# Loading three heads' results, the small columns and the function table of the output stage before the block boundary

## What is computed

```python
_, o = lax.scan(step, s0, xs)                  # recurrence over chunks, 16 value heads of 128
o = o.transpose(1, 0, 3, 2, 4).reshape(bsz, t, nh, dh)
o = rms_norm(o, norm_w) * jax.nn.silu(z.reshape(bsz, t, nh, dh).astype(f32))
y = o.reshape(bsz, t, nh * dh).astype(h.dtype) @ w_out
...
x = x + gate[:, None, :] * y
return rms_norm(x, final_g)
...                                            # second layer:
h = _rmsnorm(x, norm_pre[l])
```

## Time and profile before

| | us |
|---|---|
| median of 3 runs | 2101.82 |
| lowest and highest of them | 2099.18, 2102.6 |
| the profiled execution, its own time | 2103.15 |
| its span in the profile | 2101.4 |
| mean granted clock of TensorE in it | 0.985 |
| last write of the scan (L781) starts | 917.54 |
| first instruction of the second block | 919.88 |

### The profile page before, as it was taken

How to read it: one execution, slowest core, us unless ns; L and a number is a source line. 1 busy time by engine, 2 the same in 40 slices (tenths; PEclk the granted TensorE clock), 3 DMA queues, 4 the chain that set the end, 5 groups by cost and what they waited for, 6 DMA issues and landing times.

```text
span 2101.4 us, 29428 instructions
## 1 busy us (share of the span) xinstructions
PE 1992.7 (95%) x11256; PEld 1618.2 (77%) x11256; DVE 1272.9 (61%) x2415; ACT 853.5 (41%) x1376; POOL 138.4 (7%) x114
## 2 busy tenths in 40 slices
PE   4989999999999999969998999999999899999998
PEld 2667878888887878857776787777777678888877
DVE  6777777797869686749635644445353435633543
ACT  5644353544345443159403333544443337600321
POOL 0030202021111212000000000000000000000000
PEclk8999999999999999989999999999999999999999
DMA  7222233232323242548213211120312125211232
GB/s 282 86 75 70 87 89 106 65 101 71 105 68 105 67 120 68 168 158 287 80 41 136 66 60 41 41 101 21 111 41 81 61 72 219 91 49 41 85 116 80
DMA packets 128971, 200.27 MB, mean 95 GB/s; under 512 B 56596, under 2 KB 88084, under 8 KB 127808
## 3 DMA queue, kind: packets, MB, share of 16 engines
q1 hardware_dynamic: 128832, 198.39, 29.6%
HBM read 156.22 MB, written 42.11 MB: 94 GB/s over the span
## 4 chain that ended last, share of the span: by engine, by line
PE 47%; DVE 4%; DMA 2%; issue 2%; ACT 1%; SPq 0%; DVEq 0%; ACTq 0%
PE m_job L1682 6%; PE m_job L1684 6%; PE m_job L1683 6%; PE e_b L2369 4%; PE e_b L2371 4%; PE e_b L2370 4%; PE p_out L1352 2%; PE p_out L1353 2%; PE p_out L1354 2%; PE p_sc L1928 2%; PE p_s L1951 2%; PE e_b L2440 1%; PE e_b L2438 1%; PE e_b L2439 1%; DMA m_raw<-in_w 1%
## 5 line engine op out<-in xcount | busy, mean ns | idle before, releaser
L795 PE MATMUL p_job<-h_hi,w_hi 128*128 128x512 f32 x768 | 322.0, 419 | 18.8 <-DVE h_lo L185 17.3
L797 PE MATMUL p_job<-h_hi,w_lo 128*128 128x512 f32 x768 | 302.9, 394 | 0.0
L796 PE MATMUL p_job<-h_lo,w_hi 128*128 128x512 f32 x768 | 302.3, 394 | 0.0
L1682 PE MATMUL m_job<-h_hi,m_hi 128*128 128x512 f32 x576 | 237.6, 413 | 5.3 <-issue 4.2
L1684 PE MATMUL m_job<-h_hi,m_lo 128*128 128x512 f32 x576 | 227.4, 395 | 0.0
L1683 PE MATMUL m_job<-h_lo,m_hi 128*128 128x512 f32 x576 | 226.4, 393 | 0.0
L795 PEld LDWEIGHTS p_job<-h_hi,w_hi 128*128 128x128 f32 x768 | 146.0, 190 | 59.5 <-issue 16.2
L796 PEld LDWEIGHTS p_job<-h_lo,w_hi 128*128 128x128 f32 x768 | 146.1, 190 | 35.4 <-issue 7.9
L797 PEld LDWEIGHTS p_job<-h_hi,w_lo 128*128 128x128 f32 x768 | 145.8, 190 | 31.4
L1682 PEld LDWEIGHTS m_job<-h_hi,m_hi 128*128 128x128 f32 x576 | 108.8, 189 | 52.5 <-issue 31.0
L633 ACT ACTIVATE pre<-p_job 128x512 f32<-128x512 f32 x96 | 56.7, 591 | 179.1 <-PE p_job L797 179.1
(11 more groups left out here) (395 smaller groups left out, 4166.3 us busy)
## 6 DMA issues: line engine op xcount, KB each, us to landing
w_raw<-in_w SPq DMA_DIRECT2D x49, 512.0 KB
m_raw<-in_w SPq DMA_DIRECT2D x49, 512.0 KB, 3.8
rows<-grows SPq DMA_DIRECT2D x32, 512.0 KB, 6.6
ada<-in_ada_w SPq DMA_DIRECT2D x8, 1024.0 KB, 5.3
z_scr<-pre SPq DMA_DIRECT2D x16, 512.0 KB, 2.6
o_scr<-oT SPq DMA_DIRECT2D x64, 128.0 KB, 1.8
ob<-o_scr SPq DMA_DIRECT2D x16, 512.0 KB, 4.8
zb<-z_scr SPq DMA_DIRECT2D x16, 512.0 KB, 4.8
```

Source lines behind the costliest of these rows:

```text
L795: nc.tensor.matmul(bank, hi, h_hi[:, k, cut], start=(k == 0), stop=False)
L796: nc.tensor.matmul(bank, hi, h_lo[:, k, cut], start=False, stop=False)
L797: last = nc.tensor.matmul(bank, lo, h_hi[:, k, cut], start=False, stop=(k == KD - 1))
L1682: nc.tensor.matmul(bank, hi, h_hi[:, k, cut], start=(k == 0), stop=False)
```

## The change

`ob`, `nw`, `fg` and `np_col`, and the semaphores that count their loads, move from `stage_out` into `keep`, so that they exist in both blocks. SyncE issues the loads of `ob` for heads 0, 1 and 2 and of the three columns in the last pass of the first block, at `("merge", 0)`, behind a wait for the stores of heads 0 to 3. In the output stage the first `ob` load is that of head 3; the wait for all stores stands behind the first `zb` load. The table load at the head of `stage_out` (L1252) goes; ScalarE asks for the same table in the last pass behind the write of the last chunk but one. The SBUF reserved for descriptors, which takes its room from the same memory, is set to 1024 bytes per partition; before, the size wasn't given.

```diff
@@ stage_deltanet, SyncE's walk over the plan
+                        elif s[0] == "merge" and not s[1] and i == QK_HEADS:
+                            for q in range(2):
+                                sp.wait_ge(o_stored[q], 16 * NT)
+                            for m in range(3):
+                                sp.dma_start(keep["ob"][:, m, :], io["o_scr"][m]).then_inc(keep["o_in"][m], 16)
+                            for n, src in (("nw", "norm_w"), ("fg", "final_g"), ("np_col", "norm_pre")):
+                                sp.dma_start(keep[n][:], io[src]).then_inc(keep["cols_in"], 16)
@@ stage_deltanet, ScalarE, step "write"
                             nc.scalar.activation(oT[:, c % 2], p_query, ACT.Copy).then_inc(o_done, 1)
+                            if m == NT * QK_HEADS - 2:
+                                nc.scalar.preload_act_table_set(EXP_LN)
@@ stage_out
-        ob = sb("ob", [P, 3, T])
+        ob, nw, fg, np_col = (keep[n] for n in ("ob", "nw", "fg", "np_col"))
-        nw = sb("nw", [P, 1])
-        fg = sb("fg", [P, KD])
-        np_col = sb("np_col", [P, KD])
-        cst = sem("c_cst"); x_in = sem("c_x"); o_in = [sem(f"c_o{q}") for q in range(3)]; ...
+        cst = keep["cols_in"]; x_in = sem("c_x"); o_in = keep["o_in"]; ...
@@ stage_out, SyncE
-            load_o(0)
-            load_o(1)
-            sp.wait_ge(keep["o_stored"], 16 * QK_HEADS * NT // 2)
-            for dst, src in ((nw, io["norm_w"]), (fg, io["final_g"]), (np_col, io["norm_pre"])):
-                sp.dma_start(dst[:], src).then_inc(cst, 16)
             for m in range(len(steps)):
                 if m < V_HEADS:
                     if m >= 3:
                         sp.wait_ge(ylo_done, m - 2)
                     sp.dma_start(zb[:, m % 3, :], io["z_scr"][m]).then_inc(z_in[m % 3], 16)
-                if 2 <= m + 1 < V_HEADS:
+                if m == 0:
+                    sp.wait_ge(keep["o_stored"], 16 * QK_HEADS * NT // 2)
+                if 3 <= m + 1 < V_HEADS:
                     load_o(m + 1)
                 load_w(m)
@@ stage_out, ScalarE
-            nc.scalar.preload_act_table_set(EXP_LN)
@@ build and kernel
+            "ob": sb("ob", [P, 3, T]), "nw": sb("nw", [P, 1]), "fg": sb("fg", [P, KD]), "np_col": sb("np_col", [P, KD]),
+            "o_in": [ctx.enter_context(nc.semaphore(f"o_in{q}")) for q in range(3)],
+            "cols_in": ctx.enter_context(nc.semaphore("cols_in")),
-    nc = bacc.Bacc("TRN2", target_bir_lowering=False, num_devices=1)
+    nc = bacc.Bacc("TRN2", target_bir_lowering=False, num_devices=1, dynamic_dma_scratch_size=1024)
```

More of the change, by code:

```diff
@@ L1184, in y @@
             return middle[:, n - KD, :] if n < KD + 2 else high[:, n - KD - 2, :]
-        cst = sem("c_cst"); x_in = sem("c_x"); o_in = [sem(f"c_o{q}") for q in range(3)]; z_in = [sem(f"c_z{q}") for q in range(3)]
+        cst = keep["cols_in"]; x_in = sem("c_x"); o_in = keep["o_in"]; z_in = [sem(f"c_z{q}") for q in range(3)]
         sq_done = sem("c_sq"); sqhi_done = sem("c_sqhi"); sqlo_done = sem("c_sqlo"); ones_set = sem("c_ones"); ss_done = sem("c_ss"); ln_done = sem("c_ln"); rinv_done = sem("c_rinv")
```

## The result

| | before | changed |
|---|---|---|
| median | 2102.21 us (4 runs) | 2120.16 us (4 runs) |
| lowest and highest | 2099.18, 2106.73 | 2119.54, 2120.94 |
| profiled execution, its own time | 2103.15 | 2120.78 |
| its span | 2101.4 | 2118.9 |

The ratio is 1.0084, with a 95% interval of 1.0072 to 1.0096: the changed kernel is 17.7 us slower by the ratio, where 3.45 us less were forecast.

What follows compares the result with a forecast made beforehand. The prediction took TensorE, busy 95% of the span, as the bound, with an uncovered wait at the seam between the blocks. Its terms, −3.55 + 0.1 = −3.45 us, took the 2101.82 us median to 2098.4 us; range 2095.4 to 2101.4 us.

Steps and rivals of the forecast that it cites:

- the fourth: Whole kernel: the 1024-byte descriptor scratch and the moved buffers cost nothing, taken as 0.
- Rival 4: Whole kernel: small scratch throttles all transfers, first in the output stage's first pass; 2116 us or more, chance 0.07.
- The loads out of the seam: Between the blocks: without `ob` and column loads there, the first square starts at once, −3.55 us.
- the slack: Output stage's start: the first `zb` may land late by 3.4 us, less the second `y_lo`, without delaying the path.
- The table load in the scan: Last scan, behind the write of chunk 6: delays `vn` of chunk 7, cost +0.1 us.
- Rival 1: Table load again ahead of the first square, or a 2.66 us switch in the scan; 2.2 or 2.1 us won, chance 0.15.
- Six issues in the last pass: SyncE at merge 0 of the last pass: six issues take 2.6 us with nothing queued behind for 16 us; cost 0.
- The clock: TensorE's clock ramp behind the seam: no change on average, a scatter of 0.9 us between runs of either kernel.
- rival 2: Behind the seam: first sums at the higher clock or a ramp of 3.03 us; gain up to 5.2 us, chance 0.15.
- The sum: Whole kernel: −3.55 + 0.1 = −3.45 us, giving 2098.4 us against the median.

Runs made afterwards that it cites:

- e3_scratch: The kernel before with the descriptor scratch set to 1024 bytes alone, all tiles 15360 bytes lower, distances as before; 2102.27 us, ratio 1.0006.
- e11_pad416: The changed kernel in its own buffer order with 416 unused bytes behind `np_col`; 2098.85 us, ratio 0.9987.
- e2_before_pad32: The kernel before with 32 unused bytes per partition behind `h_lo` and nothing else; 2119.51 us, ratio 1.0087.
- e8_table_back: e5_order with the table load back at the head of the output stage and none in the scan; 2094.0 us (one run).
- e5_order: The changed kernel with the kept buffers declared ahead of `h_hi` and `h_lo`, distance 69632 bytes again; 2095.27 us, ratio 0.9974.
- e9_layout_only: e3_scratch with 12384 bytes of padding ahead of `h_hi`, giving the addresses of e5_order without the change; 2101.05 us, ratio 0.9998.
- e1: The changed kernel with 32 unused bytes per partition behind `np_col`; 2111.42 us, ratio 1.0051.
- e10: e5_order measured once more, the same kernel; 2096.44 us, ratio 0.9973.
- e6_256_64: e3_scratch padded so that weight distances from `h_hi` are a multiple of 256 in the first block and 64 in the second; 2112.0 us (one run).
- e4_offsets: e3_scratch with paddings of different sizes ahead of each weight tile, for different distances from `h`; 2112.52 us (one run).

## Why the prediction was wrong

**The step that failed** is the fourth, "the scratch of 1024 bytes and the moved buffers". It priced the scratch, which is free (e3_scratch, 1.0006), and took 0 for the whole heading; the moved buffers got no number of their own. They cost some 21 us: the twins end at +17.0, and the 3.50 won at the seam are in that; e11_pad416, with the distance mended, is 21.3 below by the medians. In the first block the distances of the `h` matmuls grew by some 13 us in sum (about 2100 of them, 6.3 ns each), of which 7.0 reached the end of the scan; the rest must have gone into waits that TensorE had anyway. In the second they grew by some 17, and 13.7 reached the end. The cover that I hadn't named was missing: TensorE is busy for 95% of the span, and few gaps are left to absorb a slower pace. It also had no rival: in all five cases, the forecast and four rivals, TensorE ran its matmuls as before but for the clock. Rival 4, slower through the scratch, has the right sign for a wrong reason. The stretch 963.4 to 983.4 of the changed kernel, which answers to the earlier trace rows, shows its place undisturbed, VectorE as full as before (19.72) and the transfers at 0.96:

```profile
963.40:983.40 20.00, 19.20 (x79) 14.54 (x79) 19.72 (x23) 18.93 (x22) 0.00 (x0) 1.00 0.96 307
```

In that first pass VectorE sets the step (the heads' period is still 5.59 us), so a slower TensorE costs almost nothing there, though its own busy time has grown (19.20 for 18.87).

The Trainium skill, "SBUF — State Buffer", section "Who interferes with whom", gives TensorE two independent read ports, one for the moving operand and one for the weight load, and says that it never waits on anyone. The rows here don't bear out that the two are independent: 227 ns become 233 to 234 when only the distance between these two operands changes (e2_before_pad32). Whether they meet in a port or in the memory behind it no run here shows.

**The loads out of the seam: right.** −3.55 forecast for the start of the square. In the changed kernel it is the block's first instruction (926.88, with `zb` issued at 926.87), `y_lo` follows, and the sums stand 3.63 us behind the start, where 3.7 was forecast. The first `zb` was 0.26 us late for its reader, well within the slack: L1416 starts at 930.62 after 0.26 us of waiting, 3.75 us behind its issue. The first `zb<-zb,rinv` starts at 935.05, 8.17 us behind the block's start; before it was 931.68 − 919.88 = 11.80, 3.63 more.

**The table load in the scan: right.** From the load to `vn` 1.29 us (921.71 to 923.00), as in the earlier trace rows; `vn` stands 1.70 us behind the write before it (921.30), before 1.58, so 0.12 late against 0.1 forecast. The drain of about 1380 ns that the Trainium skill gives for a switch ("ScalarE: Activation LUTs", section "What ACT_TABLE_LOAD costs"), and which would have made it 1.5 us late, isn't there. Rival 1 in either form is out: no load stands ahead of the first square, and e8_table_back shows what one costs.

**Six issues in the last pass: right.** SyncE's timeline of the changed kernel:

```profile
882.49 0.43 SPq L579 DMA_DIRECT2D qv<-in_ada_g  x1
883.02 2.21 SPq L589 DMA_DIRECT2D ob<-o_scr  x3
885.27 0.43 SPq L591 DMA_DIRECT2D nw<-in_norm_w  x1
885.74 0.63 SPq L591 DMA_DIRECT2D fg<-in_final_g  x1
886.41 0.49 SPq L591 DMA_DIRECT2D np_col<-in_norm_pre  x1
901.30 0.33 SPq L583 DMA_DIRECT2D z_scr<-pre  x1
```

They take 883.02 to 886.90, 3.9 us instead of my 2.6, and the queue is free for 14.4 us behind them. Between them and the end of the scan the twins of TensorE drift by 0.2 us, no more than a slower pace may make. Merge 0 starts at 881.83, ahead of them.

**The clock: as forecast, no change on average and a scatter.** In the changed kernel the low stretch (granted clock 0.5) covers the first sums as before. Behind the seam the second step of VectorE, 7.52 us before, is 7.55 in the changed kernel (940.64 to 948.19), 7.10 in e5_order and 7.19 in e11_pad416 (935.62 to 942.81). That the mended kernels gained here isn't shown: the seven traces with the old seam have 7.03 (e9) to 8.00 us (e2), the six with the new one 6.72 (e1) to 7.94 (e8). The first sum takes 0.76 to 0.77 us in all thirteen, the lower level, so that half of rival 2 came true in none. The ramp scatters by a little more than the 0.9 us allowed for, with either seam.

**The sum, without the failed step.** 3.45 us forecast; the same work with the distance mended gave 5.5, 5.7 and 2.7 us by the ratios of e5, e10 and e11 (mean 4.6), and their intervals run from 3.4 to 7.8, from 3.4 to 7.8 and from 0.6 to 4.8. At the seam the traces show 3.5 to 4.1 us, as above. What the twins of e5 and e10 gain elsewhere is no effect of the change where e9_layout_only shows it too: between 1600 and 1700 all of them gain on the profiled execution of before (e5 1.1 us, e9, e10 and e11 2.0 to 2.3), in which TensorE was idle for 2 to 3 us more. The stretch in before and in e9_layout_only:

```profile
1600.00:1700.00 100.00, 92.63 (x483) 72.24 (x482) 38.68 (x127) 35.22 (x84) 2.38 (x1) 1.00 0.25 85
```

```profile
1600.00:1700.00 100.00, 95.65 (x494) 75.36 (x493) 39.20 (x130) 35.86 (x85) 2.37 (x1) 0.98 0.24 85
```

So a comparison of two profiles flatters the mended kernels by 1 to 2 us, and that execution of before was itself 1.9 us above the median of the 23 runs. The medians don't have this flaw. Whether the order of e5 is really better than that of e11, by 2.8 us at the ratios' middle, stays open: the intervals overlap (0.9977 to 0.9984). The range of the prediction took its scatter from three runs, 2.6 us below and 0.8 above their median; the 23 runs of before lie from 4.4 below to 3.9 above theirs.

## What to carry to other kernels

A change of buffers is a change for TensorE. When tiles are added, moved or resized ahead of or between the operands of long runs of matmuls, work out the distance from the moving to the stationary tiles and keep it a multiple of 256 bytes; here the cheapest way was to declare the new buffers outside the pair. Shown is this for f32r matmuls 128x128 by 128x512 alone. When the whole is a per cent slower after an edit that touches no matmul, compare the mean durations of the matmul groups by tile names before looking for a wait, and let a kernel with a bare padding decide.

## What the runs showed of the hardware

- The pace of f32r matmuls 128x128 by 128x512 that follow at once, each with a weight load beside it, hangs on the distance in SBUF between moving and stationary tiles: 227 to 228 ns (229 to 230 in `m_job`) at multiples of 256 bytes, even and odd ones, and 232 to 235 ns at remainders of 32, 64, 96 and 128. Above 128, with equal remainders, only `y` with `h` has been seen: 232 to 236 at 160 (changed kernel), 233 to 234 at 224 (e2), but 228 to 231 at 192 (e6_256_64). Of 2102 us, 32 bytes cost 17.6. The weight loads' own mean duration moves by less than 1 ns (in `p_job` 190 before, 191 in the changed kernel).
- It is the distance, not an address: moving both operands by 32 bytes (`y` and `m` in e2_before_pad32) or all by 15360 (e3_scratch) costs nothing, and e5_order is fast with the weights where the changed kernel has them.
- With different remainders for consecutive weight tiles some pairs stay nearly fast that a rule on the matmul's own pair would call slow (`h_lo`·`m_hi`, remainder 64, 229 ns), and one is slow that it would call fast (`h_hi`·`w_lo`, remainder 0, 233 ns; both in e4_offsets). The rule for mixed distances, and whether smaller matmuls follow it, are open.
- A table load between two activations cost its 1.28 us and no drain, in the scan and at the head of the block (915.75 to 917.05). In the trace of before, 69 of the 97 loads have the next instruction of ScalarE 1.29 to 1.30 us behind their own start, and 66 of the 97 start 0.02 us behind the end of the instruction ahead of them. The instruction behind each of the other 28 waited for another engine or a transfer.
